# One block of transposes moved ahead of the second half of a matmul group, and its semaphore dropped

## The chip, the cores and the metric

The kernel runs on one core of a Trainium2 chip. The metric is the device time of one launch in microseconds (us); the median of three runs is given. The engines are TensorE (PE, matmuls; PEld is its weight load), VectorE (DVE), ScalarE (ACT), GpSimd (POOL) and SyncE (SP, which issues DMA transfers).

## The reference

One transformer-like layer over 2048 tokens of width 1024, in float32: adaptive RMS norm, a projection, sliding-window attention beside a pooling branch, an output projection, and then a mixture of experts. The last is what the change touches:

```python
scores = jax.nn.sigmoid(hf @ w_router)            # 128 experts, 8 chosen for each token
...
def expert_block(args):
    tok, rw, e = args                             # 128 token rows of one expert
    xs = hp[tok]
    y = swiglu(xs, w_gate_e[e], w_up_e[e], w_down_e[e])
    return y * rw[:, None]
routed = jnp.zeros((T + 1, D)).at[row_tok].add(y.reshape(R, D))[:T]
shared = swiglu(hf, w_sh_gate, w_sh_up, w_sh_down)
```

with `swiglu(h, wg, wu, wd) = (silu(h @ wg) * (h @ wu)) @ wd`, hidden width 256. The shared expert runs over all tokens. A last RMS norm follows.

## The kernel before

After the norm, the attention and the router, the first 990 us of the span, the kernel runs a loop over blocks of 128 token rows. There are 215 turns; the first 16 blocks are the shared expert's, the rest belong to the routed experts in order, one to a few blocks each. The loop is written with UNROLL = 8 turns in its body, each behind a test, so that every engine branches back after eight turns. There is no scheduler: each engine has its own instruction list, and semaphores tie them together.

Each fp32 product is made of three fp32r products: an operand is split into an upper part (ScalarE copies it with rounding) and a lower part (VectorE subtracts the upper from the original), and `parts` issues upper x upper, upper x lower, lower x upper for each slice of 128 of the contraction (lines L1079 to L1081). So a turn `b` has, on PE:

- 24 matmuls of 128x512 for gate and up of block b into PSUM bank B[7] (operand XR in the rows), then `gu_done`;
- 8 transposes (L962) of the next block's gathered rows into B[2] and B[3], then `xg_used`;
- the down product of the block before: 6 matmuls into B[4], 6 into B[5] (operand HR), then `y_done`;
- 2 transposes (L1110) of this block's hidden rows `hb` into B[6], behind a wait for `h_ready`, then `h_turned`.

ScalarE in a turn: loads the silu table and applies silu to the gate half (L599), copies the transposed rows to XR's upper part (L581), casts the next expert's four gate/up weight pieces if there is one (L577), copies the turned hidden rows to HR's upper part behind `h_turned` (L607), and casts two down pieces. VectorE in a turn: the product hb = silu(gate) x up (L907, `h_ready`), the lower part of XR (L893, two instructions), the lower parts of four gate/up pieces if there is a new expert (L886), then behind `y_done` and `added` the scaling of the down result out of B[4] and B[5] (L916, two instructions, `y_v`), the lower part of HR out of B[6] behind `hT_a` (L920), and two down pieces (L886). GpSimd gathers rows four blocks ahead (L450) and adds finished rows into the accumulator in device memory (L483), each such scatter behind the one before it. SP loads an expert's weights into one of two slots; a slot comes free when VectorE has made its lower parts (`v_spg`, `v_spd`).

Of the kernel before, what the change touches and what calls it, by code (L numbers as in the profile page):

```python
# [6 lines left out]
P = 128  # L7
# [103 lines left out]
def build(nc, A, out):  # L111
# [4 lines left out]
    with ctx:  # L116
# [3 lines left out]
        def sem(name):  # L120
            return ctx.enter_context(nc.semaphore(name))
# [8 lines left out]
        def C(name):  # L130
            at, w = AT[name]
            return cst[:, at:at + w]

        ident = C("ident")
# [23 lines left out]
        def take(*shape):  # L158
# [73 lines left out]
        B = [PB[:, n, :] for n in range(8)]  # L232
# [4 lines left out]
            v_cb v_mod v_trig v_wo v_x1 v_sub v_v1 v_v2 v_h2 v_P v_rank v_recs v_rope v_mx v_PT v_yT v_mask v_xn v_ch v_c16  # L237
            s_xin s_xres st_x1 st_h2 st_rec
            e_cnt e_nb e_off e_tab e_row e_thr
            w_gu w_dn a_hig a_hid v_spg v_spd rec_got rec_tr rec_go rec_win xg_z xg_r0 xg_r1 xg_r2 xg_r3 xg_used gu_done eg_done h_ready hT_a hT_sb xgT_a xgT_v y_done h_turned y_v added  # L240
            f_in0 f_in1 f_in2 f_in3 f_in4 f_sq f_v f_ln f_y f_out f_st f_g f_go f_ch""".split()
        s = {n: sem(n) for n in names}

# [6 lines left out]
        def settle(eng):  # L250

            eng.sem_inc(s["settled"], 1)
# [38 lines left out]
        hh, hl = (HR[:, n * F:(n + 1) * F].rearrange("p (k n) -> p k n", k=2) for n in range(2))  # L291
        hhf = HR[:, 0:F].bitcast(f32).rearrange("p (k n) -> p k n", k=2)
        hb = arena[:, 45568:45824]
# [199 lines left out]
        def _(act):  # L493
# [74 lines left out]
            def upper(m, pieces):  # L568

                for k in pieces:  # L570
                    if isinstance(m, int):
                        r0, w0 = (m & 1) * EW + k * PIECE, (m & 1) * (2 * EW) + k * PIECE
                        to, of = WS[:, w0:w0 + PIECE], RAW[:, r0:r0 + PIECE]
                    else:
                        r0, w0 = act.snap((m & 1) * EW + k * PIECE), act.snap((m & 1) * (2 * EW) + k * PIECE)
                        to, of = WS[:, bass.ds(w0, PIECE)], RAW[:, bass.ds(r0, PIECE)]
                    nc.scalar.copy(to, of).then_inc(s["a_hig" if k < 4 else "a_hid"], 1)  # L577

            def rows_upper():
                for n in range(2):  # L580
                    A_(xh[:, 4 * n:4 * n + 4, :], B[2 + n].rearrange("p (a b) -> p a b", a=4), ACT.Copy).then_inc(s["xgT_a"], 1)  # L581
# [7 lines left out]
            with act.Fori(0, (256 + NT) // UNROLL) as q:  # L589
                with act.If(q * UNROLL < nblk + 1):  # L590
                    for n in range(UNROLL):
                        b = act.snap(q * UNROLL + n)
                        with act.If(b < nblk + 1):


                            md = act.value_load(tab[0:1, bass.ds(b + (6 * P + 1), 1)], min_val=0, max_val=E)
                            mg = act.value_load(tab[0:1, bass.ds(b + (6 * P + 2), 1)], min_val=0, max_val=E)
                            act.wait_ge(s["gu_done"], b + 2)
                            A_(eg, B[7][:, 0:F], ACT.Silu).then_inc(s["eg_done"], 1)  # L599
                            act.wait_ge(s["xg_used"], b + 2)  # L600
                            rows_upper()
                            with act.If(mg > 0):
                                act.wait_ge(s["w_gu"], mg * 32 + 32)
                                settle(act)
                                upper(mg, range(4))
                            act.wait_ge(s["h_turned"], b + 1)
                            A_(hh, B[6][:, 0:F].rearrange("p (a b) -> p a b", a=2), ACT.Copy).then_inc(s["hT_a"], 1)  # L607
                            with act.If(md > 0):
                                act.wait_ge(s["w_dn"], md * 16 + 16)
                                settle(act)  # L610
                                upper(md, range(4, 6))
                            settle(act)
                    settle(act)
# [329 lines left out]
        def _(pe):  # L943
            mm, tr = nc.tensor.matmul, nc.tensor.transpose
            pe.wait_ge(s["v_cb"], 1)
            for m in range(12):
                pe.wait_ge(s[f"c_ada{m % NSTRIP}"], 32 * (m // NSTRIP + 1))
                W8(pe, "v_mod", m - 1)
                for k in range(KD):
                    last = mm(B[m % 2], cb[:, k, :], ada[m % NSTRIP][:, k, :], start=(k == 0), stop=(k == KD - 1))  # L950
# [7 lines left out]
            def row_transposes(src):  # L958

                cols = src.rearrange("t (p k) -> t k p", k=KD)  # L960
                for k in range(KD):
                    last = tr(B[2 + k // 4][:, (k % 4) * P:(k % 4 + 1) * P], cols[:, k, :], ident)  # L962
                last.then_inc(s["xg_used"], 1)
# [101 lines left out]
            for a in range(2):  # L1065
                for n in range(3):
                    last = tr(B[4 + a][:, n * P:(n + 1) * P], rec_rows[:, n, :].rearrange("b (t a) -> b a t", a=2)[:, a, :], ident)
# [8 lines left out]
            def parts(bank, hi, lo, w, K):  # L1076

                for k in range(K):
                    mm(bank, hi[:, k, :], w(k, 0), start=(k == 0), stop=False)  # L1079
                    mm(bank, hi[:, k, :], w(k, EW), start=False, stop=False)  # L1080
                    last = mm(bank, lo[:, k, :], w(k, 0), start=False, stop=(k == K - 1))  # L1081
                return last

            with pe.Fori(0, (256 + NT) // UNROLL) as q:
                with pe.If(q * UNROLL < nblk + 1):
                    for n in range(UNROLL):
                        b = pe.snap(q * UNROLL + n)
                        with pe.If(b < nblk + 1):
                            l1 = pe.value_load(tab[0:1, bass.ds(b + (3 * P + 1), 1)], min_val=0, max_val=E)
                            at = pe.snap((l1 & 1) * (2 * EW))  # L1090
                            pe.wait_ge(s["v_spg"], l1 + 1)
                            pe.wait_ge(s["xgT_a"], b * 2 + 2)
                            pe.wait_ge(s["xgT_v"], b * 2 + 2)
                            gu_w = lambda k, o: WS[:, bass.ds(at + o, GUW)].rearrange("p (a k n) -> p k a n", a=2, k=KD)[:, k]
                            parts(B[7].rearrange("p (a n) -> p a n", a=2), xh, xl, gu_w, KD).then_inc(s["gu_done"], 1)
                            m = n + 1
                            pe.wait_ge(s[f"xg_r{m % AHEAD}"], (q * (UNROLL // AHEAD) + (m // AHEAD + 1)) * 16)
                            row_transposes(xg[m % AHEAD])
                            l0 = pe.value_load(tab[0:1, bass.ds(b + 3 * P, 1)], min_val=0, max_val=E)
                            pe.wait_ge(s["y_v"], b + 1)  # L1100
                            pe.wait_ge(s["hT_sb"], b + 1)
                            pe.wait_ge(s["v_spd"], l0 + 1)
                            at0 = pe.snap((l0 & 1) * (2 * EW))
                            down_w = lambda c: lambda k, o: WS[:, bass.ds(at0 + (o + GUW + k * D + c * 512), 512)]
                            parts(B[4], hh, hl, down_w(0), 2)
                            parts(B[5], hh, hl, down_w(1), 2).then_inc(s["y_done"], 1)

                            pe.wait_ge(s["h_ready"], b + 1)
                            for k in range(2):
                                last = tr(B[6][:, k * P:(k + 1) * P], hb.rearrange("t (p k) -> t k p", k=2)[:, k, :], ident)  # L1110
                            last.then_inc(s["h_turned"], 1)
                    settle(pe)


# [22 lines left out]
```

## Time and profile before

| what | value |
|---|---|
| median of 3 runs | 3249.01 us (3242.24 to 3255.57) |
| profiled execution | 3249.01 us |
| its span | 3246.8 us |
| PE busy | 2886.5 us, 89% of the span |
| DVE busy | 2174.2 us, 67% |
| ACT busy | 1703.0 us, 52% |
| POOL busy | 943.7 us, 29% |

The busy time of an engine is the time in which one of its instructions ran; matmuls are pipelined, so two of them that start 0.23 us apart show 0.39 us each. "Idle before" is the time in which an engine had nothing running, and the releaser is what ended it; "issue" is a wait for nothing that the profile shows. The granted clock is a share of full speed, 2.4 GHz.

### The profile page before, as it was taken

How to read it: one execution, taken by the hardware profiler on the slowest of the kernel's cores; microseconds unless marked ns; L12 is line 12 of the kernel's file. 1: busy time of each engine (PE TensorE's matmuls, PEld its weight loads, DVE VectorE, ACT ScalarE, POOL GpSimd, SP SyncE). 2: the span in 40 equal slices, each digit the busy share in tenths (PEclk: the TensorE clock that was granted, in tenths of full speed). 3: DMA queues.
4: the chain of work that ended last, by engine and by line, in shares of the span. 5: the costliest groups of instructions: out<-in, count | busy, mean ns of one | idle time of the engine just before them, and what ended most of it. 6: DMA issues, size and time to landing. Idle time of an engine off the chain costs nothing.

```text
span 3246.8 us, 61147 instructions
## 1 busy us (share of the span) xinstructions
PE 2886.5 (89%) x13157; PEld 2198.3 (68%) x13158; DVE 2174.2 (67%) x3447; ACT 1703.0 (52%) x2435; POOL 943.7 (29%) x788
## 2 busy tenths in 40 slices
PE   6789999999838999999989989999899999999883
PEld 2355555555517888878777878777787878787772
DVE  1147666666754377677877877777777786767784
ACT  0133333333304366576766766667666675656665
POOL 0000111111132323333433433334433333333241
PEclk8899999999968999999999999999999999999996
DMA  9611111111127478798988998898989998798886
GB/s 369 186 39 52 36 42 52 39 39 52 39 59 226 102 243 260 216 293 275 323 283 291 286 307 283 272 289 277 298 277 289 278 302 257 242 283 273 284 265 233
DMA packets 160691, 690.94 MB, mean 213 GB/s; under 512 B 34097, under 2 KB 35761, under 8 KB 110610
## 3 DMA queue, kind: packets, MB, share of 16 engines
q1 hardware_dynamic: 93634, 500.17, 41.2%
q0 software_dynamic: 66896, 189.34, 26.0%
q14 instruction: 148, 1.21, 0.1%
q8 instruction: 13, 0.21, 0.0%
HBM read 587.54 MB, written 141.19 MB: 224 GB/s over the span
## 4 chain that ended last, share of the span: by engine, by line
PE 56%; DMA 17%; DVE 12%; issue 8%; ACT 3%; DVEq 2%; SPq 1%; ACTq 0%; POOL 0%; POOLq 0%
PE PB L1079 12%; PE PB L1081 11%; PE PB L1080 11%; DMA acc_tab<-arena,rec 10%; PE PB L992 9%; PE PB L962 4%; DMA RAW<-in_w_up_e 4%; PE PB L950 2%; DVE WS L886 2%; DMA arena<-in_ada_b 1%; PE PB L1051 1%; ACT WS L577 1%; DVE XR L893 1%; PE PB L1017 1%; PE PB L976 1%
## 5 line engine op out<-in xcount | busy, mean ns | idle before, releaser
L886 DVE TENSOR_TENSOR WS<-RAW,WS (+1 forms) x774 | 901.6, 1219 | 97.4 <-ACT WS L577 87.4
L577 ACT CAST WS<-RAW (+1 forms) x774 | 759.9, 1053 | 117.2 <-DMA RAW<-in_w_up_e 64.5
L483 POOL DMA_INDIRECT acc_tab<-arena,rec x215 | 409.5, 1905 | 1204.6 <-DMA acc_tab<-arena,rec 857.2
L1079 PE MATMUL PB<-WS,XR 128*128 x1720 | 701.8, 408 | 54.1 <-DVE XR L893 43.1
L1081 PE MATMUL PB<-WS,XR 128*128 x1720 | 682.1, 397 | 0.0
L1080 PE MATMUL PB<-WS,XR 128*128 x1720 | 679.4, 395 | 0.0
L1079 PEld LDWEIGHTS PB<-WS,XR 128*128 128x128 f32 x1720 | 330.6, 192 | 131.9 <-issue 69.2
L1079 PE MATMUL PB<-WS,HR 128*128 x860 | 360.6, 419 | 35.9 <-DVE HR L920 35.9
L1081 PEld LDWEIGHTS PB<-WS,XR 128*128 128x128 f32 x1720 | 328.2, 191 | 70.7
L1080 PEld LDWEIGHTS PB<-WS,XR 128*128 128x128 f32 x1720 | 329.8, 192 | 62.8
L442 POOL DMA_INDIRECT rec_tab<-recs,posi x128 | 123.7, 966 | 829.1 <-DVE recs L742 788.6
L916 DVE SCALAR_TENSOR_TENSOR arena<-PB,arena,G 128x512 f32<-128x512 f32 x430 | 302.1, 744 | 64.2 <-PE PB L1081 50.2
L1081 PE MATMUL PB<-WS,HR 128*128 x860 | 342.4, 398 | 0.0
L893 DVE TENSOR_TENSOR XR<-PB,XR 128x512 fp32r<-128x512 f32 x432 | 277.7, 684 | 94.1 <-ACT XR L581 94.1
L1080 PE MATMUL PB<-WS,HR 128*128 x860 | 340.4, 396 | 0.0
L907 DVE TENSOR_TENSOR arena<-arena,PB 128x256 f32<-128x256 f32 x215 | 90.1, 419 | 354.9 <-ACT arena L599 242.2
L450 POOL DMA_INDIRECT arena<-h_tab,rec x219 | 259.6, 1185 | 202.0 <-POOL rec L486 177.4
L599 ACT ACT_TABLE_LOAD x215 | 275.8, 1283 | 58.2 <-issue 54.2
L581 ACT ACTIVATE XR<-PB 128x512 fp32r<-128x512 f32 x432 | 234.9, 596 | 108.6 <-PE PB L962 108.6
L992 PE MATMUL PB<-arena 128*128 128x512 f32 (+1 forms) x768 | 288.6, 537 | 1.5 <-ACT arena L506 1.2
L599 ACT ACTIVATE arena<-PB 128x256 f32<-128x256 f32 x215 | 82.7, 384 | 382.7 <-PE PB L1081 381.7
L486 POOL COPY rec<-arena 128x1 int32 x215 | 262.1, 1219 | 0.0
(238 smaller groups left out, 3240.1 us busy)
## 6 DMA issues: line engine op xcount, KB each, us to landing
RAW<-in_w_gate_e SPq DMA_DIRECT2D x128, 1024.0 KB
RAW<-in_w_up_e SPq DMA_DIRECT2D x128, 1024.0 KB
RAW<-in_w_down_e SPq DMA_DIRECT2D x128, 1024.0 KB
arena<-in_ada_w SPq DMA_DIRECT2D x12, 2048.0 KB, 13.8
arena<-in_x SPq DMA_DIRECT2D x32, 512.0 KB, 3.7
h_tab<-arena SPq DMA_DIRECT2D x17, 512.0 KB, 2.9
acc_tab<-arena SPq DMA_DIRECT2D x16, 512.0 KB, 2.6
out<-fa SPq DMA_DIRECT2D x16, 512.0 KB, 5.0
```

Of the source, the lines that this page charges most:

```text
L450: g.indirect_dma_start(xg[n % AHEAD], None, h2_tab, bass.IndirectOffsetOnAxis(ap=rec[:, n % UNROLL:n % UNROLL + 1], axis=0), bounds_check= ...
L483: g.indirect_dma_start(acc_tab, bass.IndirectOffsetOnAxis(ap=rec[:, (n - 1) % UNROLL:(n - 1) % UNROLL + 1], axis=0), ys[(n - 1) % 2], None ...
L486: g.tensor_copy(rec[:, k:k + 1], rec_i[:, bass.ds(b + (AHEAD + 2), 1)]).then_inc(s["rec_win"], 1)
L577: nc.scalar.copy(to, of).then_inc(s["a_hig" if k < 4 else "a_hid"], 1)
L599: A_(eg, B[7][:, 0:F], ACT.Silu).then_inc(s["eg_done"], 1)
L886: last = V.tensor_tensor(lo, raw, hi, ALU.subtract)
L893: V.tensor_tensor(xl[:, 4 * n:4 * n + 4, :], B[2 + n].rearrange("p (a b) -> p a b", a=4), xhf[:, 4 * n:4 * n + 4, :], ALU.subtract).then_i ...
L916: last = V.scalar_tensor_tensor(out=ys[(n - 1) % 2][:, c * 512:(c + 1) * 512], in0=B[4 + c], scalar=rec_w[:, bass.ds(b, 1)], in1=G2[:, c * ...
L992: last = mm(B[4 + n][:, 0:w], xT[:, k, :], w_in[:, k, n * 512:n * 512 + w], start=(k == 0), stop=(k == KD - 1))
L1079: mm(bank, hi[:, k, :], w(k, 0), start=(k == 0), stop=False)
L1080: mm(bank, hi[:, k, :], w(k, EW), start=False, stop=False)
L1081: last = mm(bank, lo[:, k, :], w(k, 0), start=False, stop=(k == K - 1))
```

## The change

On PE the two transposes of the hidden rows and the wait for `h_ready` ahead of them are issued between the two halves of the down product, and not behind it. The semaphore `h_turned` is gone: ScalarE's copy out of B[6] waits for `y_done`, which is still raised by the last matmul of the second half. In the list of semaphore names `h_turned` is left out. No other instruction changes.

```diff
@@ -603,7 +603,7 @@
                                 act.wait_ge(s["w_gu"], mg * 32 + 32)
                                 settle(act)
                                 upper(mg, range(4))
-                            act.wait_ge(s["h_turned"], b + 1)
+                            act.wait_ge(s["y_done"], b + 1)
                             A_(hh, B[6][:, 0:F].rearrange("p (a b) -> p a b", a=2), ACT.Copy).then_inc(s["hT_a"], 1)
                             with act.If(md > 0):
                                 act.wait_ge(s["w_dn"], md * 16 + 16)
@@ -1103,12 +1103,11 @@
                             at0 = pe.snap((l0 & 1) * (2 * EW))
                             down_w = lambda c: lambda k, o: WS[:, bass.ds(at0 + (o + GUW + k * D + c * 512), 512)]
                             parts(B[4], hh, hl, down_w(0), 2)
-                            parts(B[5], hh, hl, down_w(1), 2).then_inc(s["y_done"], 1)
 
                             pe.wait_ge(s["h_ready"], b + 1)
                             for k in range(2):
-                                last = tr(B[6][:, k * P:(k + 1) * P], hb.rearrange("t (p k) -> t k p", k=2)[:, k, :], ident)
-                            last.then_inc(s["h_turned"], 1)
+                                tr(B[6][:, k * P:(k + 1) * P], hb.rearrange("t (p k) -> t k p", k=2)[:, k, :], ident)
+                            parts(B[5], hh, hl, down_w(1), 2).then_inc(s["y_done"], 1)
                     settle(pe)
```

On PE, at the end of a turn, before the change (HR is the split hidden operand, `cst,arena` the identity and the hidden rows, `h_ready` VectorE's product):

```order
L1080 MATMUL PB<-WS,HR 128x512
L1081 MATMUL PB<-WS,HR 128x512
L1110 MATMUL PB<-cst,arena 128x128 [waits h_ready]
L1110 MATMUL PB<-cst,arena 128x128
L1088 UNCONDITIONAL_BRANCH
```

and after it, from the end of the first half of the down product:

```order
L1080 MATMUL PB<-WS,HR 128x512
L1081 MATMUL PB<-WS,HR 128x512
L1109 MATMUL PB<-cst,arena 128x128 [waits h_ready]
L1109 MATMUL PB<-cst,arena 128x128
L1079 ISA
L1079 MATMUL PB<-WS,HR 128x512
```

The six matmuls of the second half, with their address instructions, have moved behind the transposes and now stand right ahead of the branch into the next turn.

On ScalarE, in the same turn, before (L607 is the copy out of B[6]):

```order
L606 REGISTER_ALU
L607 ACTIVATE HR<-PB 128x256 [waits h_turned]
L608 COMPARE_AND_BRANCH
L609 ISA
L577 REGISTER_ALU [waits w_dn]
```

and after:

```order
L606 REGISTER_ALU
L607 ACTIVATE HR<-PB 128x256 [waits y_done]
L608 COMPARE_AND_BRANCH
L609 ISA
L577 REGISTER_ALU [waits w_dn]
```

Only the semaphore of the wait differs; the two casts of down pieces (L577) stand behind it in both.

## Rows read from the trace of the kernel before

**Rows 1.** The page, part 4: shares of the chain that ended last, by engine.
```profile
PE 56%; DMA 17%; DVE 12%; issue 8%; ACT 3%; DVEq 2%; SPq 1%; ACTq 0%; POOL 0%; POOLq 0%
```

**Rows 2.** Stretches of the loop: us, busy us (x instructions) by engine, clock, DMA.
```profile
996.00:1147.00 151.00, 151.00 (x745) 127.52 (x744) 66.37 (x106) 60.70 (x92) 43.93 (x47) 1.00 0.52 123
1147.00:3188.60 2041.60, 1919.98 (x9105) 1599.34 (x9104) 1531.16 (x1947) 1331.07 (x1746) 762.41 (x596) 0.98 0.88 276
```

**Rows 3.** Timeline of PE, early product: start us, busy us, engine, line, operation.
```profile
2004.25 0.49 PE L1079 MATMUL PB<-WS,HR 128*128 x1
...
2005.73 0.39 PE L1079 MATMUL PB<-WS,HR 128*128 x1
...
2006.86 0.40 PE L1081 MATMUL PB<-WS,HR 128*128 x1
2007.10 0.39 PE L1110 MATMUL PB<-cst,arena 128*128 128x128 f32 x2
...
2007.56 0.39 PE L1080 MATMUL PB<-WS,XR 128*128 x1
```

**Rows 4.** Timeline of all engines in that iteration, VectorE's and ScalarE's rows.
```profile
2004.02 0.42 DVE L907 TENSOR_TENSOR arena<-arena,PB 128x256 f32<-128x256 f32 x1 [0.21 <-ACT arena L599]
...
2007.52 0.75 DVE L916 SCALAR_TENSOR_TENSOR arena<-PB,arena,G 128x512 f32<-128x512 f32 x1 [1.11 <-PE PB L1081]
2007.53 0.39 ACT L607 ACTIVATE HR<-PB 128x256 fp32r<-128x256 f32 x1 [1.95 <-PE PB L1110]
```

**Rows 5.** Timeline of PE, late product; in brackets idle us before, and releaser.
```profile
1986.24 0.39 PE L1079 MATMUL PB<-WS,HR 128*128 x1
...
1987.61 0.39 PE L1110 MATMUL PB<-cst,arena 128*128 128x128 f32 x2
1988.48 0.49 PE L1079 MATMUL PB<-WS,XR 128*128 x1 [0.48 <-DVE XR L893]
1988.81 0.39 PE L1080 MATMUL PB<-WS,XR 128*128 x1
```

**Rows 6.** Timeline of VectorE in the iteration of rows 5.
```profile
1986.51 0.41 DVE L907 TENSOR_TENSOR arena<-arena,PB 128x256 f32<-128x256 f32 x1
...
1988.04 1.41 DVE L916 SCALAR_TENSOR_TENSOR arena<-PB,arena,G 128x512 f32<-128x512 f32 x2
...
1994.67 0.42 DVE L907 TENSOR_TENSOR arena<-arena,PB 128x256 f32<-128x256 f32 x1 [2.33 <-ACT arena L599]
```

**Rows 7.** Timeline of PE at a loop boundary.
```profile
2046.96 0.50 PE L1110 MATMUL PB<-cst,arena 128*128 128x128 f32 x2 [0.87 <-DVE arena L907]
2048.47 0.49 PE L1079 MATMUL PB<-WS,XR 128*128 x1 [1.01 <-DVE XR L893]
2048.80 0.39 PE L1080 MATMUL PB<-WS,XR 128*128 x1
```

**Rows 8.** Timeline of VectorE at three loop boundaries.
```profile
1459.45 0.42 DVE L907 TENSOR_TENSOR arena<-arena,PB 128x256 f32<-128x256 f32 x1 [6.56 <-issue]
...
2046.48 0.42 DVE L907 TENSOR_TENSOR arena<-arena,PB 128x256 f32<-128x256 f32 x1 [6.53 <-issue]
...
2541.20 0.42 DVE L907 TENSOR_TENSOR arena<-arena,PB 128x256 f32<-128x256 f32 x1 [6.50 <-issue]
```

**Rows 9.** Waits of the whole span: us in total, times, longest us.
```profile
DVE arena L907 <- issue: 112.8, 25, 6.6
...
PE PB L1079 <- DVE XR L893: 43.1, 68, 2.3
...
PE PB L1110 <- DVE arena L907: 34.0, 21, 3.9
```

**Rows 10.** Waits, same columns, around the scatter-add.
```profile
POOL acc_tab L483 <- DVE arena L916: 280.7, 45, 14.1
...
DVE arena L916 <- DMA acc_tab<-arena,rec: 13.5, 6, 4.7
```

**Rows 11.** Stretches behind rows 7: PE busy (x instructions), granted clock, DMA.
```profile
2050.00:2053.00 3.00, 3.00 (x8) 0.50 1.00 197
```

More of the change, by code:

```diff
@@ L239, in build @@
             e_cnt e_nb e_off e_tab e_row e_thr
-            w_gu w_dn a_hig a_hid v_spg v_spd rec_got rec_tr rec_go rec_win xg_z xg_r0 xg_r1 xg_r2 xg_r3 xg_used gu_done eg_done h_ready hT_a hT_sb xgT_a xgT_v y_done h_turned y_v added
+            w_gu w_dn a_hig a_hid v_spg v_spd rec_got rec_tr rec_go rec_win xg_z xg_r0 xg_r1 xg_r2 xg_r3 xg_used gu_done eg_done h_ready hT_a hT_sb xgT_a xgT_v y_done y_v added
             f_in0 f_in1 f_in2 f_in3 f_in4 f_sq f_v f_ln f_y f_out f_st f_g f_go f_ch""".split()
```

## The prediction

> **What bounds the kernel now.** I read the page first, then the stretches, then whole iterations of the expert loop. One iteration is one turn `b` of the loop that all four engines run. The profiled execution took 3249.01 us, of which the trace spans 3246.8; the three timed runs have the same median, 3249.01, so the sum is made against 3249. The page's chain of waits gives PE 56% of the span, DMA 17% and VectorE 12% [rows 1]. By stretches the loop runs from 996 to 3188.6 us, which for the 214 periods between its 215 iterations is 10.2 us each. In the first 151 us (the shared expert, tokens in order) PE has no idle time, with the clock at full; in the 2041.6 us after that it is busy 1920 us [rows 2]. So about 122 us of idle PE and some microseconds of low clock are all that anything in this loop can still give or take cheaply.
>
> Three kinds of iteration show where that idle time sits. They differ by when VectorE's product `hb` (L907), which releases the two transposes of the hidden rows (L1110), is ready.
>
> Early: the first down matmul starts at 2004.25, the second half's at 2005.73, the twelfth at 2006.86, the transposes at 2007.10, the second matmul of the next gate/up at 2007.56 [rows 3]. L907 had ended at 2004.44 [rows 4], so both orders find it done. One wrinkle matters for the count: 128x512 matmuls follow each other by 0.23 us, but the second one behind a pair of transposes comes 0.46 us after the pair's start.
>
> Late: L907 ends at 1986.92 because VectorE first finished two pieces of weights [rows 6]. The old transposes (1987.61) still do not wait for it, but the second half's first down matmul (1986.24) lies ahead of it. PE then idles 0.48 us for the subtracted rows of L893 [rows 5].
>
> Loop boundary: every eighth iteration VectorE idles some 6.5 us for nothing that the profile names, L907 ends at 2046.90 [rows 8], PE idles 0.87 us before L1110 and 1.01 us before the gate/up matmuls, which again wait for L893 [rows 7].
>
> Going through all iterations by those two times, I count 130 early, 59 late and 25 at the boundary with a next iteration (the last has none). Rows 3, 5 and 7 are one of each. The wait totals fit: PE lost 34.0 us in 21 waits for L907 at the transposes, and 43.1 us in 68 waits for L893 at the next gate/up [rows 9]. The transposes are therefore followed, wherever their wait is long, by a second wait for a later instruction of the same VectorE sequence.
>
> **The change, part by part.** The two transposes and their wait for `h_ready` move from behind the twelve down matmuls to between the sixth and the seventh. Nothing is added on PE; one semaphore increment goes.
>
> First, PE where the product is early (130 iterations). The same instructions run in another order with the same two switches into transposes. Old: from the first down matmul to the second gate/up 2007.56 - 2004.25 = 3.31 us. New: 1.48 to the end of half one, then transposes to the second matmul behind them 0.46 (2007.56 - 2007.10), four more steps of 0.23 and one into gate/up and one to its second matmul: 1.48 + 0.46 + 6 x 0.23 = 3.32. Cost 0.01, which I set to nothing; the cover is the 1.29 us between L907's end and 2005.73.
>
> Second, PE where it is late. The second half of the down product (1.37 us) is now held, but it fills time that PE spent waiting for L893. From the end of L907, old: the boundary's second gate/up starts at 2048.80, 1.90 us later; the late one at 1988.81, 1.89 us later [rows 5, 7]. New: 0.06 from L907's end to the first transpose (2046.96), then 0.46 and 6 x 0.23, 1.90 us. So there is nothing to win, and to lose only what the hand-over costs: the pair of transposes is busy 0.50 us when it starts from a wait and 0.39 when it does not [rows 3, 7], 0.11 more, plus rounding, 0.13. In a late iteration in which VectorE also splits the next gate/up weights, the next product comes from VectorE's own queue and the 0.13 is hidden. That leaves the 31 late ones without that work and the 25 at the boundary: 56 x 0.13 = 7.3 us. Bounds: 0, and 84 x 0.13 = 10.9.
>
> Third, who waits for PE. `y_done` now comes behind everything, and ScalarE's copy of the turned rows (L607) waits for it too, where it used to wait for the transposes. With an early product both consumers start 0.24 us later: L916 began 0.66 us after the start of the twelfth down matmul (2007.52 - 2006.86), and that matmul moves by the length of the pair, 2007.10 - 2006.86. For L607 the old release was 0.43 behind the transposes' start, the new one 0.66 behind a matmul that starts at that same time, again 0.23. With a late product, L916 moves from 1988.04 to L907's end + 0.06 + 0.46 + 4 x 0.23 + 0.66 = 1989.02, by about 0.97 us, and L607 alike. VectorE's next instruction that PE needs is L907 of the next iteration, and it has 2.33 us of idle time ahead of it there [rows 6], so 0.97 is absorbed. Behind L916 queue L920 and two weight pieces; behind L607 the two casts for them. PE wants these only at the next down matmuls, 9.4 us after the last ones in an undisturbed turn ([rows 2]: 151 us for some 16).
>
> It is not absorbed where the iteration is the last of eight. There VectorE runs the same short sequence, stands for 6.5 us, and only then delivers L907, on which PE waits [rows 8]. I take that gap to start when its sequencer has passed the last wait of the eighth iteration (ScalarE's casts, behind L607), so a shift of L607 passes through. There are four such ends with a late product and nothing to hide it (the next L907 at 1459.45, 2046.48, 2541.20 and, between them, one near 1878), 4 x 0.96 = 3.8, and three with an early product (near 1062, 1966 and 2207), 3 x 0.24 = 0.7. At the others VectorE is still splitting weights when `y_done` comes, or L916 waits for the scatter. Together 4.6 us; bounds 0 (the gap starts by itself earlier) and 26 boundaries x 0.96 = 25.
>
> The Trainium skill speaks for passing it through: "Runtime: NRT & Kernel Launch", section "Instruction fetch mechanics", says that a taken branch to a target outside the small instruction window must fetch by DMA before execution goes on. This trace has 25 such idle times of VectorE before L907, 112.8 us [rows 9]. If the fetch started ahead of the branch instead, the sum would lose its 4.6.
>
> Fourth, the scatter-add. GpSimd's scatter waits for L916 in 45 of 215 cases, and L916 in turn waited for a scatter only 6 times [rows 10]. I give it nothing, with 6 x 0.97 = 6 as the upper bound. The very last one is 0.24.
>
> Sum: 7.3 + 4.6 + 0.2 = 12 us. About a quarter of the loop is paced by something else (the chain gives DMA 17% of the span [rows 1]), and there a PE delay vanishes: 9 us remain. 3249 + 9 = 3258 us, 0.3% slower, which lies within 0.5% (16 us), about what a measurement of this kernel can tell from no change.
>
> **The rivals.** (a) Longer single gaps bring the clock down more often: slower. At the boundary PE's two gaps, 0.87 and 1.01 us with transposes between them [rows 7], become one of about 2.3. Soon after the old pair of gaps the granted clock was 0.50, which is 1.2 instead of 2.4 GHz [rows 11]; eight matmuls then came 0.43 us apart instead of 0.23, 1.6 us lost. I count such a fall at 13 of 24 boundaries of the routed stage. If the one long gap makes it happen at all, 11 x 1.6 = 18 us on top: 3276. Against it: the idle time in that stretch is the same in total. It decides if a fall follows the gap at more than ten further boundaries. (b) The shift of L607 and L916 reaches the weight loads: the casts and splits of the down pieces release the slot for the next load, and at 0.88 of DMA share [rows 2] late loads are not made up. 31 late iterations x 0.97 = 30 us if all count: 3279, and with my sum behind it 3288. Against it: the idle 2.33 us of VectorE, and busy stretches have iterations in which nothing shifts. (c) Faster: at eight boundaries the product is late in the eighth iteration, and PE's first gate/up comes 1.5 us behind the transposes, not 0.87; the branch now runs under six matmuls. Worth 8 x 0.5 = 4 us, and if my 0.13 and 0.96 terms are nothing, 3245. If in truth the wait for L893 were bookkeeping and PE gained all 34 us of its waits for L907, 3215; [rows 5, 7] speak against it: L1079 names L893 as what ended its idle time in both. (d) Nothing reaches the end: 3249.
>
> **How the numbers follow.** Forecast with (d) within 16 us: 0.77. Rival (a) 0.10, (b) 0.07, (c) 0.06, half of it a small gain that is still no measurable change. Slower by over 0.5% needs (a), (b) or the upper bounds of two terms: 0.18. Faster by over 0.5%: 0.04. Within: 0.78. The range takes in (c)'s small gain, 3242, and most of (a), 3276.
>
> **What would show it.** In the new profile: waits for L907 at the transposes grow from 34 us to 34 plus up to 1.37 for each boundary and some 0.7 for each late iteration, about 100 us, while the waits for L893 at gate/up fall to nearly nothing; the sum of both and the time of the loop hardly move. L916 waits for PE far more often than 45 times. The last gap of VectorE before L907 at the four boundaries stays 6.5 us and L907 comes 1 us later against its down matmuls. I am wrong if the idle time of PE in the loop changes by over 20 us, or if the low-clock stretches double.

## The result, and the profile after

The changed kernel takes 3277.7 us (3270.3 to 3280.6, 6 runs) where the kernel before takes 3251.6 on the same chip: a ratio of 1.0076, 95% interval 1.0058 to 1.0093. Measured again on another chip the ratio was 1.0053 (1.0037 to 1.0070). The forecast was 3258, 0.3% slower, most likely within 0.5% of before (0.78); slower by more than that had a chance of 0.18, and it is what came. The sign was right. The time lies 1.7 us above 3276, the upper figure that the prediction names for its range; put on the 3249 us of the prediction by the ratio it is 3273.7. The loss is two to three times the 9 us forecast.

The span grew from 3246.8 to 3268.3 us, and all of it in the loop. The same stretch of it, from 1147 us to the last product, with the same 9105 matmuls as the second line of [rows 2]:

```profile
1147.00:3210.00 2063.00, 1932.39 (x9105) 1581.49 (x9104) 1533.70 (x1947) 1332.12 (x1747) 744.58 (x596) 0.98 0.87 274
```

It is 2063.0 us long against 2041.6, 21.4 more, at the same mean clock of 0.98. PE's busy time in it grew by 12.4 us and its idle time by 9.0, although the matmuls are the same: they show 0.39 us each where full pace is 0.23, so the first 0.16 us of a delay between two of them count as busy. PE's waits, whole span (total us, times, longest), beside [rows 9] and [rows 10]:

```profile
PEld PB L1109 <- DVE arena L907: 116.2, 81, 5.2
DVE arena L907 <- issue: 113.8, 25, 7.3
...
DVE arena L916 <- PE PB L1081: 106.3, 83, 2.8
...
PE PB L1109 <- DVE arena L907: 81.7, 62, 4.8
...
PE PB L1079 <- issue: 10.3, 18, 1.3
...
DVE arena L916 <- DMA acc_tab<-arena,rec: 6.6, 4, 2.0
...
PE PB L1079 <- DVE XR L893: 2.3, 1, 2.3
```

The waits for L907 at the transposes rose from 34.0 to 81.7 us and those for L893 at the gate/up product fell from 43.1 to 2.3, as forecast; together 77 before and 84 now. That is only 7 us, so these two waits do not hold the loss. What does is seen in one late turn, the one of [rows 5]. PE:

```profile
1995.66 0.40 PE L1081 MATMUL PB<-WS,HR 128*128 x1
1996.61 0.50 PE L1109 MATMUL PB<-cst,arena 128*128 128x128 f32 x2 [0.55 <-DVE arena L907]
1996.86 0.48 PE L1079 MATMUL PB<-WS,HR 128*128 x1
1997.18 0.40 PE L1080 MATMUL PB<-WS,HR 128*128 x1
...
1998.10 0.39 PE L1081 MATMUL PB<-WS,HR 128*128 x1
1998.61 0.49 PE L1079 MATMUL PB<-WS,XR 128*128 x1
1998.94 0.39 PE L1080 MATMUL PB<-WS,XR 128*128 x1
```

and VectorE there, against [rows 6]:

```profile
1996.13 0.42 DVE L907 TENSOR_TENSOR arena<-arena,PB 128x256 f32<-128x256 f32 x1
1996.46 1.28 DVE L893 TENSOR_TENSOR XR<-PB,XR 128x512 fp32r<-128x512 f32 x2
1998.74 1.41 DVE L916 SCALAR_TENSOR_TENSOR arena<-PB,arena,G 128x512 f32<-128x512 f32 x2 [0.99 <-PE PB L1081]
```

L907 ends at 1996.55 and the transposes follow at once. The last down matmul starts at 1998.10 and the first gate/up matmul 0.51 us behind it, where full pace is 0.23; nothing is named for it. L893 had ended at 1997.74, 0.87 us earlier, so it is not what held it (before, that distance was 0.36). From the end of L907 to the second gate/up matmul it is 2.39 us; in [rows 5] 1.89. I had worked out 1.90 for both orders, and 0.13 on top.

Going through all 214 periods of both traces, turn by turn, each from a turn's first down matmul to that of the next:

| turns of the kernel before | number | longer now, us in all | mean |
|---|---|---|---|
| early product | 130 | -0.8 | 0.0 |
| late, the first of a run of late ones | 34 | 15.3 | 0.45 (median 0.50) |
| late, behind a late one | 11 | 2.0 | 0.2 (median 0.0) |
| late, held up by weight loads (over 11 us before) | 14 | 0.9 | 0.1 |
| first of a loop pass (boundary) | 25 | 4.1 | 0.2 |
| sum | 214 | 21.5 | |

In a run of late turns the half microsecond is lost once: the next product comes from VectorE's own queue at the same time as before. The second measurement's trace has the same table: -1.3, 16.2, 1.4, -3.3 and 2.4. Single boundary turns differ by up to 3.5 us either way, so only the second row is firm; it stands for 15 to 16 us of a loss of 16 to 26, and the rest stays open. The split between early and boundary turns also hangs on where a period is cut. Cut at the second gate/up matmul it is -11.6 and 22.0: the distance from L907's end to the second gate/up grew from 1.93 to 2.96 us at the boundary (medians), and most of that comes back before the next down product. At the boundary shown under rival (a) below, the low clock falls on the down matmuls where it used to fall on the gate/up matmuls behind them.

### The profile page after: what moved, and what is told of

The parts are those of the page before. It is cut to its first block, busy times and chain, and to the rows that moved or that the text cites. A ratio compares the mean times of both kernels' runs of the same rounds, so it can differ in the third digit from the quotient of the medians.

```text
span 3268.3 us, 61147 instructions
## 1 busy us (share of the span) xinstructions
PE 2897.1 (89%) x13157; PEld 2179.6 (67%) x13158; DVE 2177.0 (67%) x3447; ACT 1703.9 (52%) x2435; POOL 925.3 (28%) x788
## 4 chain that ended last, share of the span: by engine, by line
PE 59%; DMA 12%; DVE 12%; issue 9%; ACT 4%; DVEq 2%; SPq 1%; ACTq 1%; POOL 1%; POOLq 0%
PE PB L1079 12%; PE PB L1081 12%; PE PB L1080 12%; PE PB L992 9%; DMA acc_tab<-arena,rec 6%; DMA RAW<-in_w_up_e 4%; PE PB L962 4%; DVE WS L886 2%; PE PB L950 2%; ACT WS L577 2%; PE PB L1109 2%; DMA arena<-in_ada_b 2%; PE PB L1051 1%; PE PB L1017 1%; PE PB L976 1%
## 5 line engine op out<-in xcount | busy, mean ns | idle before, releaser
L577 ACT CAST WS<-RAW (+1 forms) x774 | 760.1, 1053 | 116.0 <-DMA RAW<-in_w_up_e 64.7
L1079 PE MATMUL PB<-WS,XR 128*128 x1720 | 684.2, 398 | 18.1 <-issue 10.0
L1081 PE MATMUL PB<-WS,XR 128*128 x1720 | 675.6, 393 | 0.0
L1080 PE MATMUL PB<-WS,XR 128*128 x1720 | 674.4, 392 | 0.0
L1079 PE MATMUL PB<-WS,HR 128*128 x860 | 384.5, 447 | 33.1 <-DVE HR L920 32.8
L1079 PEld LDWEIGHTS PB<-WS,XR 128*128 128x128 f32 x1720 | 327.0, 190 | 119.0 <-issue 52.8
L916 DVE SCALAR_TENSOR_TENSOR arena<-PB,arena,G 128x512 f32<-128x512 f32 x430 | 302.5, 746 | 112.9 <-PE PB L1081 106.3
L1081 PEld LDWEIGHTS PB<-WS,XR 128*128 128x128 f32 x1720 | 325.4, 189 | 68.2
L1080 PEld LDWEIGHTS PB<-WS,XR 128*128 128x128 f32 x1720 | 326.4, 190 | 66.0
L1081 PE MATMUL PB<-WS,HR 128*128 x860 | 348.7, 405 | 0.0
L1080 PE MATMUL PB<-WS,HR 128*128 x860 | 346.1, 402 | 0.0
L893 DVE TENSOR_TENSOR XR<-PB,XR 128x512 fp32r<-128x512 f32 x432 | 278.1, 686 | 95.4 <-ACT XR L581 95.4
L907 DVE TENSOR_TENSOR arena<-arena,PB 128x256 f32<-128x256 f32 x215 | 90.4, 420 | 333.5 <-ACT arena L599 219.3
L486 POOL COPY rec<-arena 128x1 int32 x215 | 253.8, 1180 | 0.0
```

What stands on the lines that cost most here:

```text
L486: g.tensor_copy(rec[:, k:k + 1], rec_i[:, bass.ds(b + (AHEAD + 2), 1)]).then_inc(s["rec_win"], 1)
L893: V.tensor_tensor(xl[:, 4 * n:4 * n + 4, :], B[2 + n].rearrange("p (a b) -> p a b", a=4), xhf[:, 4 * n:4 * n + 4, :], ALU.subtract).then_i ...
L916: last = V.scalar_tensor_tensor(out=ys[(n - 1) % 2][:, c * 512:(c + 1) * 512], in0=B[4 + c], scalar=rec_w[:, bass.ds(b, 1)], in1=G2[:, c * ...
```

## The experiments

Three theories stood. S: PE's sequencer, the part that takes the instructions in order and hands them to the array, stands at the late wait; it must afterwards issue what lies behind it, six matmuls with their register instructions, before it can start the head of the next turn (branch, table load, register work); the head is then late. H: handing over from transposes that started out of a wait costs the array or the weight path half a microsecond. R: the later release of L607 and L916 costs it. In the figures below "late distance" is the time from the end of L907 to the second gate/up matmul, the median of the late turns outside the boundary (48 to 52 of them). "First late turns" are the 34 of the table's second row. "Loop" is the time from the first down matmul of the first turn to that of the last, in the profiled execution: 2192.5 us before, 2214.1 and 2207.9 in the two traces of the changed kernel.

**The sequencer's own rows.** The traces hold the sequencer's instructions too, and they settle much of this by themselves. Asked by line (`--source`), `PEldq` rows are those of PE's sequencer (duration in ns, least, median and most; first and last start in us). L1088 is the test and branch ahead of the next turn, L1089 the table load. Turn 98 before, where L907 ended at 1986.92, and in the changed kernel, where it ended at 1996.55:

```profile
L1088 PEldq COMPARE_BRANCH  x1: 68/68/68, 1987.1 to 1987.1; - x1
L1089 PEldq TENSOR_LOAD <-cst x1: 306/306/306, 1987.3 to 1987.3; - x1
```

```profile
L1088 PEldq COMPARE_BRANCH  x1: 68/68/68, 1997.2 to 1997.2; - x1
L1089 PEldq TENSOR_LOAD <-cst x1: 308/308/308, 1997.5 to 1997.5; - x1
```

The branch comes 0.15 us behind L907's end before and 0.65 behind it now. In the old order it runs while the array still has two down matmuls to start: the sequencer is ahead of the array, and `h_ready` held it even in turns in which the transposes on the array did not wait. The same in all kernels below, median of 50 late turns (without the boundary and the eighth turns), us:

| kernel | matmuls behind the transposes | L907's end to the branch | branch to the first gate/up weight load |
|---|---|---|---|
| before | 0 | 0.15 | 1.40 |
| three matmuls behind the wait | 3 | 0.40 | 1.40 |
| changed, both traces | 6 | 0.65 | 1.40 |
| all twelve behind the wait | 12 | 1.40 | 1.62 |
| changed, load moved, two traces | 6 | 0.65, 0.68 | 0.90 |
| before, load moved, both traces | 0 | 0.15 | 1.39 |
| before, second load | 0 | 0.15 | 2.06 |
| before, both limits lifted | 0 | 0.15 | 0.79 |

In none of these kernels does the branch's distance vary by more than 0.03 us among the 50 turns. So S's half microsecond can be read off directly: the head takes the same 1.40 us and starts 0.50 us later.

**The semaphores without the order.** The order of before, the release of the change:

```diff
-parts(B[5], hh, hl, down_w(1), 2).then_inc(s["y_done"], 1)
+parts(B[5], hh, hl, down_w(1), 2)
 ...
-last.then_inc(s["h_turned"], 1)
+last.then_inc(s["y_done"], 1)
 ...
-act.wait_ge(s["h_turned"], b + 1)
+act.wait_ge(s["y_done"], b + 1)
```

> The order of the kernel before, but y_done is raised by the last transpose and ScalarE's copy waits for it: the semaphores of the change without its order. Theory S (TensorE's sequencer: behind a late h_ready it must still issue the six matmuls before it can start the head of the next turn, branch and table load, and that delays the next gate/up by 0.5 us): no order changed, so late turns keep 1.89 us from the end of L907 to the second gate/up matmul, and the time stays within 4 us of before, 3248 to 3256. Rival R (the later release of L607 and L916 is what costs the 22 us): here they are released 0.24 us later in every turn, so some 5 to 10 us slower, 3257 to 3262.

The ratio to before was 1.0021 (0.9976 to 1.0067), on a chip that scattered from 3265 to 3326 us for the kernel before: no verdict by time. That scatter lies largely ahead of the loop, whose first down matmul came at 1025 to 1063 us in the four profiled executions of this chip and at 996 before. By turns there is a verdict. Late distance 1.89 us, unchanged, and the 34 first late turns cost -0.4 us in all. R is out for them. The loop was 2198.8 us, 6.3 more than before, spread over all kinds of turn.

**The table load ahead of the wait, in the changed kernel.** The register that tells the next gate/up product its weight slot is loaded before the down product and not in the next turn's head:

```diff
-l1 = pe.value_load(tab[0:1, bass.ds(b + (3 * P + 1), 1)], min_val=0, max_val=E)
+l1 = pe.snap(l1_reg, min_val=0, max_val=E)
 ...
 l0 = pe.value_load(tab[0:1, bass.ds(b + 3 * P, 1)], min_val=0, max_val=E)
+pe.reg_mov(l1_reg, pe.value_load(tab[0:1, bass.ds(b + (3 * P + 2), 1)], min_val=0, max_val=E))
```

> The changed kernel, with the table load for the next turn's gate/up (TENSOR_LOAD and its register instructions) issued ahead of the wait for h_ready and kept in a register. Theory S: the head of a turn becomes short enough to hide under the six matmuls; in late turns the second gate/up comes 2.0 instead of 2.39 us behind L907's end, the last down matmul is followed at once (0.46 instead of 0.84 us to the second gate/up), and the time falls by 10 to 20 us to 3258 to 3268. Rival H (the array's or the weight path's hand-over from transposes that started out of a wait costs the 0.5 us): nothing changes, 3277. Rival R: 3277.

> The changed kernel with the table load of the next turn issued ahead of the wait, again, since the chip of the first call scattered by 2%. Theory S, from the turns measured so far: the 34 late turns that open a run of late ones cost 15 to 16 us more than before in the changed kernel and 1 us here; so 0.0 to 0.3% over before, against 0.5 to 0.8% for the changed kernel. Rival H and R: 0.5 to 0.8% as the changed kernel.

First chip: 1.0012 (0.9980 to 1.0045), second: 1.0027 (1.0007 to 1.0047), where the changed kernel had 1.0053 and 1.0076, on two other chips. The late distance was 2.02 us on both. PE in the same turn (98) of the second run; here L1113 are the transposes, L1082 to L1084 the matmuls:

```profile
2005.73 0.51 PE L1113 MATMUL PB<-cst,arena 128*128 128x128 f32 x2 [0.55 <-DVE arena L907]
2006.00 0.47 PE L1082 MATMUL PB<-WS,HR 128*128 x1
...
2007.23 0.39 PE L1084 MATMUL PB<-WS,HR 128*128 x1
2007.46 0.39 PE L1082 MATMUL PB<-WS,XR 128*128 x1
2007.69 0.40 PE L1083 MATMUL PB<-WS,XR 128*128 x1
```

The first gate/up matmul now follows the last down matmul at full pace, 0.23 us, behind the same wait, the same transposes and the same six matmuls. H is out: nothing that the array does differs. The first late turns cost 1.1 us in all in the first run and 1.4 in the second, against 15.3 and 16.2. In both runs other turns were longer than before (boundary +7.3 and +8.8, load-bound +4.4 and +7.3, early +4.4 and +7.1), which the change of the load does not explain and which I leave open. With them the loop of the two profiled executions is 2212.1 and 2218.6 us, no shorter than that of the changed kernel (the second was the slowest of its twelve, 15.5 us over their median). So the late turns are shown to be cured; that the whole time is cured is not. By time, the second ratio and the 1.0053 have intervals that overlap.

**The same load moved in the kernel before.** The same edit on the old order:

> The same table load moved ahead in the kernel before. Theory S: late turns wait for L893 there, so their 1.89 us stay; only the eighth turn's 2.57 us falls, and VectorE's gap at the boundary hides that. Time within 4 us of before, 3248 to 3256. If the load ahead of the down product delays something of its own, slower; if the sequencer limits more turns than I think, faster by up to 10 us.

> The kernel before with the same load moved ahead, again. Theory S: late turns wait for L893, nothing to win except in the eighth turns, whose successors wait for VectorE's gap: within 0.2% of before.

1.0008 (0.9985 to 1.0031) and 1.0004 (0.9987 to 1.0020). Late distance 1.88 us; in the eighth turns of the loop it fell from 2.57 to 1.88, and VectorE's gap hid it. So the load costs nothing in the old order; it is the change that makes it matter. With a shorter head the first gate/up weight load stays 1.39 us behind the branch (1.40 before): here L893 sets it, and in the kernel before the head and L893 end within 0.01 us of each other.

**Three matmuls behind the wait and not six.** The transposes stand behind the ninth down matmul:

```diff
 parts(B[4], hh, hl, down_w(0), 2)
+mm(B[5], hh[:, 0, :], dw(0, 0), start=True, stop=False)
+mm(B[5], hh[:, 0, :], dw(0, EW), start=False, stop=False)
+mm(B[5], hl[:, 0, :], dw(0, 0), start=False, stop=False)
 pe.wait_ge(s["h_ready"], b + 1)
 ...
-parts(B[5], hh, hl, down_w(1), 2).then_inc(s["y_done"], 1)
+mm(B[5], hh[:, 1, :], dw(1, 0), start=False, stop=False)
+mm(B[5], hh[:, 1, :], dw(1, EW), start=False, stop=False)
+mm(B[5], hl[:, 1, :], dw(1, 0), start=False, stop=True).then_inc(s["y_done"], 1)
```

> The changed kernel with the transposes behind nine of the twelve down matmuls instead of six, so three matmuls stand between the wait and the head. Theory S: half of the sequencer's 0.5 us, the second gate/up 2.1 to 2.15 us behind L907's end in late turns, and about half of the 26 us lost, 3260 to 3268. Rival H: still 0.5 us for each late turn, 3277. Rival R: L607 and L916 are released in late turns 0.7 us earlier than in the changed kernel, so under it also about half; R is told apart by e2 and e3.

0.9992 (0.9950 to 1.0034), again on the scattering chip: no verdict by time. Late distance 2.15 us, and the first late turns cost 8.2 us in all: half of both. The loop was 2207.0 us. In the same turn 98 the profile names L893 for the idle time before gate/up:

```profile
2057.93 0.46 PE L1113 MATMUL PB<-cst,arena 128*128 128x128 f32 x2
...
2058.69 0.40 PE L1116 MATMUL PB<-WS,HR 128*128 x1
2059.65 0.50 PE L1079 MATMUL PB<-WS,XR 128*128 x1 [0.56 <-DVE XR L893]
2059.98 0.39 PE L1080 MATMUL PB<-WS,XR 128*128 x1
```

but L907 had ended at 2057.83 and L893 by the usual 1.2 us behind it, 0.6 us before the matmul. With the six of the change and none in the old order the points are 1.89 or less, 2.15, 2.39: about 0.25 us of sequencer time for three matmuls, which is what the branch shows (0.15, 0.40, 0.65).

**A second load in the head, old order.** No matmul moves, the head is longer:

```diff
 at = pe.snap((l1 & 1) * (2 * EW))
-pe.wait_ge(s["v_spg"], l1 + 1)
+l1b = pe.value_load(tab[0:1, bass.ds(b + (3 * P + 1), 1)], min_val=0, max_val=E)
+pe.wait_ge(s["v_spg"], l1b + 1)
```

> The kernel before with a second, equal table load in the head of each turn. Theory S: the head (1.56 us from L907's end to the first gate/up in late turns) gets longer by one load, some 0.3 to 0.6 us, and since it is already level with the wait for L893 there, late turns go from 1.89 to 2.2 to 2.5 us although no matmul has moved; early turns keep 9.35 us.

One execution: 3298.1 us, 44 us over before. Late distance 2.54 us, 0.65 more, just above the 2.2 to 2.5 expected; the head takes 0.66 more. Early turns grew by 0.03 us each. Turn 98, and the waits:

```profile
2014.35 0.39 PE L1111 MATMUL PB<-cst,arena 128*128 128x128 f32 x2
2015.86 0.49 PE L1079 MATMUL PB<-WS,XR 128*128 x1 [1.12 <-issue]
2016.19 0.40 PE L1080 MATMUL PB<-WS,XR 128*128 x1
```

```profile
PE PB L1079 <- issue: 78.9, 67, 2.8
...
PE PB L1079 <- DVE HR L920: 34.4, 11, 4.8
...
PE PB L1079 <- DVE XR L893: 22.2, 19, 2.3
```

A wait without a name, 78.9 us in 67 cases (11.0 us in 10 before), has appeared where before it was L893. This is S by itself: late turns in the old order stand just at the edge, where the head and L893 end together.

**All twelve behind the wait.**

```diff
-parts(B[4], hh, hl, down_w(0), 2)
 pe.wait_ge(s["h_ready"], b + 1)
 ...
+parts(B[4], hh, hl, down_w(0), 2)
 parts(B[5], hh, hl, down_w(1), 2).then_inc(s["y_done"], 1)
```

> The changed kernel with the transposes ahead of all twelve down matmuls. Then even an early product (0.23 us behind the start of the down matmuls) is waited for, and a late one (2.1 us) holds all twelve. In late turns PE itself needs 0.06 + 0.46 + 12 x 0.23 = 3.28 us from L907's end to the second gate/up, more than the sequencer's 1.89 + 4 x 0.26 = 2.9: 3.3 us. Early turns lose 0.3 to 0.8 us each, late ones 1.4: 3249 + 130 x 0.5 + 59 x 1.4 + 25 x 1.4 = 3430, between 3380 and 3460. If instead the place does not matter (rival H: 0.5 us in each turn that waits), 130 + 84 turns x 0.5 = 107, 3356.

One execution: 3383.1 us, at the lower edge of what was expected. PE waits 188.0 us for L907 at the transposes, and the distance, over all turns outside the boundary, is 3.47 us, near the 3.3 worked out for the array itself. So the place does matter, beyond what S and H dispute about.

**The changed kernel again**, on one chip with the next two:

> The changed kernel itself, beside before and beside the variants of this call on one chip. Theory S: 0.76% over before as first measured, with late turns at 2.39 to 2.40 us from L907's end to the second gate/up. If that ratio does not return on this chip, the 22 us hang on the chip and only the 0.5 us of each late turn are the change's.

1.0053 (1.0037 to 1.0070), late distance 2.39 us. The half microsecond returned; of the 0.76% some two thirds did, and the interval does not reach it.

**More turns in the loop's body.** UNROLL = 16 and 68 in place of 8, old order:

> The kernel before with sixteen turns in the loop's body instead of eight: half the branches back. If VectorE's 6.5 us gap before L907 belongs to the branch back, it occurs at 13 instead of 26 turns, and about half of the 95 us by which the boundary turns exceed 9.35 us go, some 35 to 45 us, 1.1 to 1.4% faster. If the gap comes by the amount of instructions read (each so many kilobytes), its number stays, and the time stays within 0.3%.

> The same with 68 turns in the body: 3 branches back. By the branch theory some 65 to 80 us faster, 2.0 to 2.5%. By the amount theory no change.

By time both theories failed: 1.0073 (1.0045 to 1.0102) and 1.0102 (1.0079 to 1.0125). With sixteen turns the loop was 2226.2 us, 33.7 longer. VectorE's gap before L907 all but went (13.0 us, 3 cases), and PE got one of its own at each of the 13 branches back; those turns take 16 to 20.6 us, more than before. Waits of the sixteen-turn kernel, then its instruction queues and those of before (packets, MB, share):

```profile
PE PB L1079 <- issue: 67.3, 16, 8.1
...
DVE arena L907 <- issue: 13.0, 3, 7.8
```

```profile
q8 instruction: 159, 2.61, 0.3%
q14 instruction: 234, 1.92, 0.2%
```

```profile
q14 instruction: 148, 1.21, 0.1%
q8 instruction: 13, 0.21, 0.0%
```

One instruction queue moves 2.61 MB where it moved 0.21, and with 68 turns again 159 packets and 2.61 MB, although it branches back 3 times and not 13. With 68 turns the loss is not in the loop: in the profiled execution, the slowest of six, that took 2188.8 us, 3.7 less than before, where the branch theory wanted 65 to 80 less. What follows took 115.5 us and not 58.3, and there VectorE and ScalarE wait 71.4 and 57.1 us once. The last pass of this body has over 50 turns that are tested and skipped; that these take the time would fit, but was not tried.

**Both limits of a late turn lifted, old order.** If S holds, the kernel before has two limits at one place: the head and the second half of L893. The load moved ahead lifts one, a split wait the other:

```diff
-pe.wait_ge(s["xgT_a"], b * 2 + 2)
-pe.wait_ge(s["xgT_v"], b * 2 + 2)
+pe.wait_ge(s["xgT_a"], b * 2 + 1)
+pe.wait_ge(s["xgT_v"], b * 2 + 1)
 ...
+if k == KD // 2:
+    pe.wait_ge(s["xgT_a"], b * 2 + 2)
+    pe.wait_ge(s["xgT_v"], b * 2 + 2)
```

The last three lines stand in the loop over k of the gate/up product; the load is moved ahead as above.

> The kernel before with the table load moved ahead and the wait of the gate/up product split: its first twelve matmuls wait for the first half of XR alone (one L893), the other twelve for the second. By theory S late turns in the kernel before have two limits at the same place, the head of the turn (some 1.56 us behind L907's end) and L893's second half (1.55); the load moved ahead lifts the first, the split the second. The second gate/up should then come 1.25 to 1.35 us behind L907's end at the loop boundary and at the transposes' own pace, 1.2, in late turns, 0.6 us less than before in some 70 turns of which about 60 stand on the path: 25 to 40 us faster, 0.8 to 1.2%. If the head of a turn was no limit of its own, or the wait for L893 was bookkeeping, late turns stay at 1.9 us and the time within 0.2%.

0.9935 (0.9909 to 0.9961), 3298.9 us against 3321.9 on that chip: 0.65% faster than the kernel before, though by less than the 0.8 to 1.2% expected. The loop of the profiled execution was 2164.2 us, 28.3 less than before, within the 25 to 40 expected. Late distance 1.28 us, and at the boundary 1.31 for 1.92. Turn 98:

```profile
2053.22 0.40 PE L1086 MATMUL PB<-WS,HR 128*128 x1
2053.46 0.39 PE L1120 MATMUL PB<-cst,arena 128*128 128x128 f32 x2
2053.61 0.47 PE L1084 MATMUL PB<-WS,XR 128*128 x1
2053.92 0.39 PE L1085 MATMUL PB<-WS,XR 128*128 x1
```

Now the gate/up product follows the transposes as in an early turn [rows 3].

## Why the prediction was right in sign and short in size

**Early turns, nothing.** Right: 130 turns, -0.8 us; the transposes stand 1.47 us behind the first down matmul, as worked out.

**Late turns, 0.13 us in 31 of them and in 25 at the boundary, 7.3 us.** This is the step that failed. The size was 0.5 us and not 0.13, and it fell on the 34 turns that open a run of late ones: 17 us with those behind them. I had counted what PE executes between L907's end and the second gate/up matmul, and not what its sequencer must issue in that time. The order of instructions shows it: between the wait and the next turn's branch there were two transposes, and now six matmuls with their register instructions as well. I had said that L893 set the end of a late turn in both orders; it did in the old one, where the head stood about level with it, and in the new one the head does. Moving the load (late distance 2.39 to 2.02), halving the matmuls (2.15) and doubling the load in the old order (1.89 to 2.54) each move it by what S says. My 1.90 + 0.13 is what the changed kernel does once the load is out of the way: 2.02. The half of the step that says a run of late turns hides the loss held, except for its first turn. The wait also stood wrong in the prediction: it asked when the transposes on the array would wait, and in the old order they did not; but the sequencer did wait for L907 there, and its branch came 0.15 us behind it in all 50 late turns looked at. What makes the product late in the turn of [rows 5, 6], which those rows do not show, is this row of VectorE, right ahead of L907:

```profile
1984.24 2.35 DVE L886 TENSOR_TENSOR WS<-RAW,WS  x2
```

**The signs named beforehand.** PE's waits for L907 grew to 81.7 us (about 100 forecast) and those for L893 all but went, as said. Both signs of being wrong failed to catch the error: the idle time of PE in the loop grew by 9.0 us, not by over 20, since part of each delay counts as busy, and the low-clock stretches did not double. What did move was the time of the loop, by 21.4 us, where it was to "hardly move".

**Release of L916 and L607.** Right. In the turn shown L916 starts 2.19 us after L907's end against 1.12 in [rows 6], later by 1.07 (0.97 forecast), and it waited for PE 83 times, not 45. That its delay reaches nothing fits the table: early turns, which have it too, are no longer.

**The last turns of a pass, 4.6 us.** Right in the mean for the four with a late product. The time from their first down matmul to the end of the next L907 was 14.47 to 14.57 us before. Over the four traces in the new order (the changed kernel twice, the moved load twice) it averages 15.34, 0.83 more, where I had 0.96; the single values run from 14.89 to 16.03. In the two traces of the old order with the load moved it averages 14.49, from 14.22 to 14.95. One of the four in the changed kernel, against [rows 8]:

```profile
2044.19 0.42 DVE L907 TENSOR_TENSOR arena<-arena,PB 128x256 f32<-128x256 f32 x1
...
2048.53 2.36 DVE L886 TENSOR_TENSOR WS<-RAW,WS  x2
2058.15 0.42 DVE L907 TENSOR_TENSOR arena<-arena,PB 128x256 f32<-128x256 f32 x1 [7.26 <-issue]
```

The gap itself varies, here 7.26 us, so where the shift enters is not shown. For the three with an early product the shift of 0.24 is not to be seen in that scatter. Boundary turns are 4.1 us longer in all (2.4 in the second trace), where 25 x 0.13 and the 4.6 make 7.9.

**Rival (a), the clock.** Wrong. At this boundary PE stands still for 3.25 us in one piece, and the clock falls:

```profile
2054.98 0.39 PE L1081 MATMUL PB<-WS,HR 128*128 x1
2058.62 0.51 PE L1109 MATMUL PB<-cst,arena 128*128 128x128 f32 x2 [3.25 <-DVE arena L907]
2058.89 0.47 PE L1079 MATMUL PB<-WS,HR 128*128 x1
...
2060.31 0.63 PE L1081 MATMUL PB<-WS,HR 128*128 x1
2060.73 0.69 PE L1079 MATMUL PB<-WS,XR 128*128 x1
```

but the slowed matmuls are the last down ones, where before they were gate/up ones. Stretches at the lower level behind 1000 us: 20 in both traces, 138 us before and 136 after, the last one of each behind the loop's end.

**Rival (b), the weight loads.** Not seen: the 14 load-bound turns grew by 0.9 us, in the second trace they shrank by 3.3. **Rival (c), eighth turns 0.5 us shorter.** Wrong, for the reason of the failed step: it let the branch run under six matmuls, but the branch has to wait until they are issued. Their distance grew from 2.57 to 3.07. **The absorbed quarter, 3 us.** No such share of the sum was: 15.3 + 2.0 + 0.9 + 4.1 - 0.8 is the whole 21.5. What was absorbed is the half microsecond of the 25 other late turns, 2.9 us instead of 12.5.

## What to carry to other kernels

A wait can cost more than the idle time of the array behind it. Here it held PE's whole instruction list, and what the sequencer must do before the next useful instruction (branch, table load, register work, 1.40 us) started only once everything between had been issued (0.50 us for six matmuls). In this kernel a wait that may be late is better placed ahead of little, and the late turns gained when the register load of the next turn stood ahead of it; the old order, with nothing behind the wait, is still the faster of the two. To see such a limit, look for the sequencer's branch and loads in the trace, and compare the end of the instruction that is named as releaser with the start of what it is said to have released: 0.36 us where L893 and the head ended together, 0.6 to 0.9 where it was the head alone. Where two limits of a stretch end at the same time, a change that shows no loss for one of them can run into the other; here lifting the head's limit alone gave nothing and lifting both gave 0.65%. Lifting L893's alone was not tried.

## What was not expected of the hardware

Six down matmuls of 128x512 with their register instructions take PE's sequencer 0.50 us (three of them 0.25, twelve 1.25), against 1.37 us for six on the array. The table load itself runs 0.31 us; with the register work around it a second one made the head 0.66 us longer, and moving the only one away made it 0.50 shorter. The branch back after sixteen turns held PE where after eight it did not, and one instruction queue's traffic went from 0.21 to 2.61 MB. That the instructions of eight turns were read once and those of a longer body in every pass would fit both figures, but it was not tried by itself.
